# Sparse attention of the two later mixers: groups taken one by one, or in pairs around halves of the merge gates

## The reference, cut to what matters

```python
def nsa_mixer(q, kv, gate_logits, cmp_pos, cmp_w1, cmp_w2):   # 8 heads = 2 kv x 4, d = 64, S = 256
    ...                                   # kc, vc: 15 compressed keys and values
    def block_fn(qb):                     # 128 queries
        p_c = masked_softmax(q . kc - slope * dist)           # compressed branch
        o_c = p_c . vc
        ...                               # 16 blocks selected of 4: all of them
        p_s = masked_softmax(q . ks - slope * dist);  o_s = p_s . vs   # selected branch
        p_w = masked_softmax(q . kw - slope * dist);  o_w = p_w . vw   # window branch
        return g[..., 0:1] * o_c + g[..., 1:2] * o_s + g[..., 2:3] * o_w
...
g_a, g_b, g_c = split(sigmoid(h @ w_merge_gate[l] + b_merge_gate[l]), 3)   # 1024 x 3072
mix = g_a * (y_a @ w0) + g_b * (y_b @ w1) + g_c * (y_c @ w2)
```

## Time and profile before

| | |
|---|---|
| median of 3 runs | 1881.63 us (1881.41 to 1882.01) |
| the profiled execution | 1882.02 us; span 1880.2 us |
| PE busy | 1863.6 us (99%) |
| PEld busy | 1601.1 us (85%) |
| DVE busy | 1340.4 us (71%) |
| ACT busy | 861.0 us (46%) |
| POOL busy | 124.3 us (7%) |
| DMA | 343.46 MB, mean 183 GB/s |
| TensorE clock granted, mean | 0.999 of full |

### The profile page before, as it was taken

How to read it: one execution, slowest core, us unless ns; L and a number is a source line. 1 busy time by engine, 2 the same in 40 slices (tenths; PEclk the granted TensorE clock), 3 DMA queues, 4 the chain that set the end, 5 groups by cost and what they waited for, 6 DMA issues and landing times.

```text
span 1880.2 us, 28201 instructions
## 1 busy us (share of the span) xinstructions
PE 1863.6 (99%) x10664; PEld 1601.1 (85%) x10664; DVE 1340.4 (71%) x1697; ACT 861.0 (46%) x1107; POOL 124.3 (7%) x155
## 2 busy tenths in 40 slices
PE   9999999999999999999999999999999999999998
PEld 8998888888888888888977888888888897788887
DVE  5676767776767776776876677677777767677777
ACT  5554434474334444344375433443335337644333
POOL 1001200230000100000300100010000020000000
PEclk9999999999999999999999999999999999999999
DMA  7423555425555565544434465556554444455453
GB/s 307 180 90 148 199 181 187 171 82 203 212 191 188 224 223 200 181 167 169 178 137 162 175 227 184 201 218 229 197 182 175 164 166 168 147 189 213 180 199 113
DMA packets 48548, 343.46 MB, mean 183 GB/s; under 512 B 5472, under 2 KB 5504, under 8 KB 8784
## 3 DMA queue, kind: packets, MB, share of 16 engines
q1 hardware_dynamic: 43200, 310.92, 45.5%
q0 software_dynamic: 5264, 31.35, 4.4%
HBM read 341.20 MB, written 1.05 MB: 182 GB/s over the span
## 4 chain that ended last, share of the span: by engine, by line
PE 66%; issue 0%; DVE 0%; POOL 0%; ACT 0%; DVEq 0%; POOLq 0%
PE bank L1068 16%; PE bank L856 12%; PE bank L858 12%; PE bank L857 12%; PE bank L1067 7%; PE bank L919 2%; PE bank L1070 1%; PE bank L1147 1%; PE bank L1519 1%; PE bank L964 1%; PE bank L959 1%; PE bank L960 1%; PE bank L1443 0%; PE bank L1381 0%; PE bank L1508 0%
## 5 line engine op out<-in xcount | busy, mean ns | idle before, releaser
L2065 DVE TENSOR_TENSOR wlo<-raw,whi 128x2048 fp32r<-128x2048 f32 x292 | 672.1, 2304 | 223.2 <-ACT whi L1586 222.7
L1586 ACT ACTIVATE whi<-raw 128x2048 fp32r<-128x2048 f32 x293 | 559.3, 1910 | 256.4 <-PE bank L858 252.3
L1068 PE MATMUL bank<-ysp,whi 128*128 128x512 f32 x1920 | 666.1, 396 | 0.0
L1067 PE MATMUL bank<-ysp,wlo 128*128 128x256 f32 x1680 | 468.6, 279 | 0.0
L1068 PEld LDWEIGHTS bank<-ysp,whi 128*128 128x128 f32 x1920 | 347.7, 188 | 67.0
L1067 PEld LDWEIGHTS bank<-ysp,wlo 128*128 128x128 f32 x1680 | 316.8, 189 | 10.7
L1669 ACT ACTIVATE sg<-sg 128x256 f32<-128x256 f32 x120 | 50.2, 418 | 468.2 <-DVE sg L2262 468.2
L856 PE MATMUL bank<-whi,ysp 128*128 128x512 f32 (+3 forms) x592 | 217.3, 367 | 0.3 <-DVE wlo L2065 0.3
L858 PE MATMUL bank<-whi,ysp 128*128 128x512 f32 (+3 forms) x592 | 212.8, 359 | 0.0
L857 PE MATMUL bank<-wlo,ysp 128*128 128x512 f32 (+3 forms) x592 | 212.4, 359 | 0.0
L856 PE MATMUL bank<-whi,hl 128*128 128x512 f32 x528 | 206.0, 390 | 0.0
(11 more groups left out here) (359 smaller groups left out, 2356.7 us busy)
## 6 DMA issues: line engine op xcount, KB each, us to landing
raw<-stream SPq DMA_DIRECT2D x294, 1024.0 KB, 4.8
sr<-side POOLq DMA_DIRECT2D x10, 1024.0 KB, 5.2
gbc<-gains POOLq DMA_DIRECT2D x11, 512.0 KB, 3.9
cw<-small POOLq DMA_DIRECT2D x2, 2048.0 KB, 10.7
gbias<-gate_rows POOLq DMA_DIRECT2D x6, 512.0 KB, 4.3
dbias<-dilb POOLq DMA_DIRECT2D x1, 2304.0 KB, 12.8
lng<-rows POOLq DMA_DIRECT2D x2, 1024.0 KB, 5.2
tab<-second POOLq DMA_DIRECT2D x1, 1724.0 KB, 15.0
```

Source lines behind the costliest of these rows:

```text
L1067: pe.matmul(o[:, 0, :], lo[:, k, cols], yh[:, k, :], start=False, stop=False, skip_group_check=True)
L1068: last = pe.matmul(o, hi[:, k, cols], ysp[:, :, k, :], start=k == 0, stop=k == 7)
L1586: act.activation(whi[s], raw[s], ACT.Copy).then_inc(hi_made, 1)
L2065: dve.tensor_tensor(wlo[s], raw[s], whi[s].bitcast(F32), ALU.subtract).then_inc(lo_made, 1)
```

## The change

The stage's own order replaces `attention` on all three engines. TensorE, for k from 0 to 4: scores of the two groups of pair k (with one wait, for the maxima of all groups of the pair before), gate half 2+2k, turning of both groups of pair k-1, gate half 3+2k, value sums of both groups of pair k-1. ACT: split of tile 4+2k, copies of pair k-1, tanh of half 2+2k, exponentials of group 2k, split of tile 5+2k, exponentials of group 2k+1, scaling of both, tanh of half 3+2k; for k = 3 the high part of the first output (`out_high(0)`) comes first. DVE: split of tile 4+2k, (k = 0: maxima of groups 0 and 1), sum of gate half 2+2k, copies of pair k-1, (k = 1 to 3: maxima of pair k), shares of group 2k, sum of gate half 3+2k, split of tile 5+2k, shares of group 2k+1. Buffers, banks, amounts of work and the code of each step stay as they were.

```diff
--- before.py
+++ after.py
@@ -1492,9 +1492,6 @@
                 square(B, plan.tb["ya"], lambda m, k: uA[:, m, k * P:k * P + P], 4, 8)
                 pe.wait_ge(ro_used, l + 1)
 
-                def gate_step(i):
-                    gate_half(2 + i, i < 2)
-
                 def compressed_out(m):
 
                     if m == 0:
@@ -1520,7 +1517,39 @@
                                              start=False, stop=i % 4 == 3 and kt == m, tile_position=(0, r), skip_group_check=True)
                     return last
 
-                attention(B, "nsa", nsa_groups(), AG_NSA + 8 * l, gate_step, summed=values_summed)
+                groups, ag = nsa_groups(), AG_NSA + 8 * l
+                tb_nsa = [plan.tb["nsa"] + (i if i < 4 else 2 * i - 4) for i in range(9)]
+
+                def pair_scores(k):
+
+                    pe.wait_ge(mx_ready, ag + 2 * k)
+                    for i in (2 * k, 2 * k + 1):
+                        g = groups[i]
+                        for h in range(4):
+                            o = pb[2 + 2 * (i % 2) + h // 2][:, (h % 2) * S:(h % 2) * S + g["nk"]]
+                            last = pe.matmul(o, g["q"][h], g["k"][h], start=True, stop=True)
+                        last.then_inc(sc_done, 1)
+
+                def pair_T(k):
+
+                    for i in (2 * k, 2 * k + 1):
+                        g, nt = groups[i], groups[i]["nk"] // P
+                        for b in range(nt):
+                            hs = range(4) if nt == 1 else (2 * b, 2 * b + 1)
+                            pe.wait_ge(p_ready, 2 * (ag + i) + (2 if nt == 1 else b + 1))
+                            batch(B, tb_nsa[i] + b, [g["p"][:, h, kt * P:kt * P + P] for h in hs for kt in range(nt)])
+
+                for k in range(5):
+                    if k < 4:
+                        pair_scores(k)
+                    gate_half(2 + 2 * k, k == 0)
+                    if k:
+                        pair_T(k - 1)
+                    gate_half(3 + 2 * k, k == 0)
+                    if k:
+                        for i in (2 * k - 2, 2 * k - 1):
+                            copied(B, tb_nsa[i + 1])
+                            values_summed(i).then_inc(o_done, 1)
 
                 tb = plan.tb["y"]
                 pe.wait_ge(yb_ready, l + 1)
@@ -1998,13 +2027,46 @@
                     act.wait_ge(o_done, AG_NSA + 8 * l + 4 * m + 4)
                     act.activation(cTh[m], pb[1].rearrange("p (h q) -> p h q", h=4), ACT.Copy).then_inc(oT_hi, 1)
 
-                def beside(i):
-
-                    if i == 6:
+                groups, ag = nsa_groups(), AG_NSA + 8 * l
+                tb_nsa = [plan.tb["nsa"] + (i if i < 4 else 2 * i - 4) for i in range(8)]
+
+                def exps(i):
+
+                    g = groups[i]
+                    act.wait_ge(mx_ready, ag + i + 1)
+                    for h in range(4):
+                        p = g["p"][:, h, 0:g["nk"]]
+                        ins = act.activation(p, p, ACT.Exp, bias=nmx[:, i % 2, h:h + 1], accum_out=den[:, i % 4, h:h + 1])
+                    ins.then_inc(p_made, 1)
+
+                def scaled(i):
+
+                    g = groups[i]
+                    act.wait_ge(share_ready, 8 * l + i + 1)
+                    for h in range(4):
+                        p = g["p"][:, h, 0:g["nk"]]
+                        ins = act.activation(p, p, ACT.Copy, scale=share[:, i % 2, h:h + 1])
+                        if h % 2:
+                            ins.then_inc(p_ready, 1)
+
+                for k in range(5):
+                    if k == 3:
                         out_high(0)
-                    ahead(B, "gates", 2 + i)
-
-                attention(B, "nsa", nsa_groups(), AG_NSA + 8 * l, beside, lambda i: gate_tanh(2 + i), shared=8 * l)
+                    ahead(B, "gates", 2 + 2 * k)
+                    if k:
+                        for i in (2 * k - 2, 2 * k - 1):
+                            if i >= 2:
+                                act.wait_ge(o_done, ag + i - 1)
+                            for b in range(groups[i]["nk"] // P):
+                                plain_T(B, tb_nsa[i] + b, pt_part(groups[i], b))
+                    gate_tanh(2 + 2 * k)
+                    if k < 4:
+                        exps(2 * k)
+                        ahead(B, "gates", 3 + 2 * k)
+                        exps(2 * k + 1)
+                        scaled(2 * k)
+                        scaled(2 * k + 1)
+                        gate_tanh(3 + 2 * k)
                 ahead(B, "gates", 11)
                 gate_tanh(11)
 
@@ -2774,21 +2836,47 @@
                     dve.wait_ge(oT_hi, M * l + m + 1)
                     dve.tensor_tensor(cTl[m], pb[1].rearrange("p (h q) -> p h q", h=4), cTh[m].bitcast(F32), ALU.subtract).then_inc(oT_lo, 1)
 
-                def beside(i):
-
-                    if i == 6:
+                ag = AG_NSA + 8 * l
+                tb_nsa = [plan.tb["nsa"] + (i if i < 4 else 2 * i - 4) for i in range(8)]
+
+                def maxima(i):
+
+                    g, nk_ = groups[i], groups[i]["nk"]
+                    dve.wait_ge(sc_done, ag + i + 1)
+                    dve.wait_ge(p_ready, 2 * (ag + i) - 2)
+                    if i >= 2:
+                        dve.wait_ge(tb_done, B.tb0 + tb_nsa[i - 2] + groups[i - 2]["nk"] // P)
+                    for h2 in range(2):
+                        src = bank2(2 + 2 * (i % 2) + h2)[:, :, 0:nk_]
+                        ins = dve.tensor_tensor(g["p"][:, 2 * h2:2 * h2 + 2, 0:nk_], src, g["bias"][h2], ALU.add)
+                    link(ins)
+                    link(dve.tensor_reduce(mx[:, i % 2, :], g["p"][:, :, 0:nk_], AX_X, ALU.max))
+                    dve.tensor_scalar(nmx[:, i % 2, :], mx[:, i % 2, :], -1.0, None, ALU.mult).then_inc(mx_ready, 1)
+
+                for k in range(5):
+                    if k == 3:
                         out_low(0)
-                    if i % 2 or i >= 8:
-                        gate_sum(2 + i)
-                        if i < 8:
-                            shares(groups[i], i)
-                        ahead(B, "gates", 2 + i)
-                    else:
-                        ahead(B, "gates", 2 + i)
-                        gate_sum(2 + i)
-                        shares(groups[i], i)
-
-                attention(B, "nsa", groups, AG_NSA + 8 * l, None, beside)
+                    ahead(B, "gates", 2 + 2 * k)
+                    if k == 0:
+                        maxima(0)
+                        maxima(1)
+                    gate_sum(2 + 2 * k)
+                    if k:
+                        for i in (2 * k - 2, 2 * k - 1):
+                            if i >= 2:
+                                dve.wait_ge(o_done, ag + i - 1)
+                            for b in range(groups[i]["nk"] // P):
+                                plain_T(B, tb_nsa[i] + b, pt_part(groups[i], b))
+                    if 0 < k < 4:
+                        maxima(2 * k)
+                        maxima(2 * k + 1)
+                    if k < 4:
+                        shares(groups[2 * k], 2 * k)
+                    gate_sum(3 + 2 * k)
+                    if k < 4:
+                        ahead(B, "gates", 3 + 2 * k)
+                        shares(groups[2 * k + 1], 2 * k + 1)
+                ahead(B, "gates", 11)
                 tb = plan.tb["y"]
                 square_T(B, tb, 2, bTl, bTh)
                 b0 = plan.step["branch"]
```

## The result

The changed kernel takes 1903.08 us (median of 4 runs, 1900.77 to 1903.87) against 1881.74 us of before; the ratio is 1.0112, 95% interval 1.0099 to 1.0124. It is slower by 21 us. The profiled execution took 1900.77 us, span 1899.0.

A forecast was written before the change was run, and what follows sets the result against it. TensorE, busy 99% of the span, was taken as the bound. Stages 9.15 us longer per layer (18.3) on 1882.02 gave 1900.3, median 0.4 lower; clock falls of 3.4 us made 1903, range 1894 to 1911.

The forecast's parts named there:

- both stages without the clock: Stage in both layers, clock kept up: each 9.15 us longer, 18.3 us for two.
- the clock: TensorE's clock drops to half pace in stalls of 3 us: 1.7 us a fall, one counted per layer, 3.4 us.
- The order on ACT and DVE: Splits stand ahead of work TensorE needs; it waits about 3, 3.4 and 3.3 us at three places a layer.
- (a): Gate half 3+2k shares bank 0, waits for DVE's sum of half 2+2k; about 3 us at gate half 5.
- (b): From pair 2, turning's third and fourth batches wait for ACT's and DVE's copies; stalls 3.4 us (pair 2), 3.3 (pair 3).
- Pair 3's stall: TensorE's wait in the turning of pair 3: 3.3 us, able to swallow a clock fall in pair 2's stall.
- Wait (c): Scores of a pair wait for maxima of the pair before; not late, maxima done at 6.2 us, scores after 6.8.
- The switches: Fewer switches on TensorE save 0.3 us per each of four pairs plus 0.3, about 1.5 us a layer (0 to 4.5).
- Not slower: Rival, 5%: the order fits, turning waits shrink to the bank's turn-round, 2.4 us in all, switches pay 3.0: 1881 us.
- The clock falls in every stall: Rival, 15%: the clock drops in all three stalls a layer, loss behind pair 3 adding 3.4 us: 1907 us.

The follow-up runs named there:

- the first run: Changed kernel with DVE's split of tile 4+2k moved behind the gate sum and copies in loops 1, 3 and 4: 1888.78 us, ratio 1.0038.
- the third: Changed kernel with ACT's split of tile 4+2k moved ahead of the scaling, for k from 1: 1893.27 us, ratio 1.0063.
- the fourth: The order in step: changed kernel with ACT and DVE reordered, TensorE's pairs kept: 1880.72 us, ratio 0.9996 to the kernel before.

## Why the prediction was right

It said 1903 us, slower; 1903.08 was measured. The path it walked is right piece by piece; that the total agrees to a tenth is in part luck, since its last two terms were off in opposite directions. Step by step, with the measured moments moved by the 0.22 us by which this stage began sooner:

| step | forecast | measured |
|---|---|---|
| gate half 5 starts | 956.2 | 956.13 |
| turning of pair 1 done | 972.4 | 972.33 |
| turning of pair 2 done | 992.1 | 991.75 |
| turning of pair 3 done | 1011.3 | 1010.91 |
| stage ends | 1018.9 | 1018.43 |
| both stages without the clock | +18.3 | +17.4 (86.06 + 86.05 kept busy in all waits, less 154.68) |
| the clock | +3.4 | +3.9 (the rest of 1903.08 - 1881.74) |

*The order on ACT and DVE.* Waits (a) and (b) came where they were forecast and for the reason given: the first run shows it by taking DVE's split out of the way, the third by making ACT's sooner, the fourth by both. Pair 3's stall was 1.8 us, not 3.3, because the late end of gate half 9 used up the rest, as forecast for a fall there; with the clock kept up it was 3.4 (fourth batch 3.10 us behind the third). Wait (c), the scores, was not late. ACT's idle time ahead of the first tanh was to be some 6 us:

```profile
942.61 0.64 ACT L2010 ACTIVATE gates<-gates 128x512 f32<-128x512 f32 x1 [6.24 <-DVE gates L2805]
```

*The switches* were put too low. By an estimate from the order in step (76.87 us, less two turn-rounds of 0.6 and two waits of 0.15 at the gate halves) a layer with TensorE unhindered would take 75.4, so the pairs save 2.0 us, not 1.5. The chains hide that in the changed kernel: the piece that TensorE paces, from gate half 5 to the end of pair 1's turning, took 16.20 us against the 16.2 of the forecast.

*The clock* was the weakest step. The prediction took the price of a fall from TensorE's pace at the beginning of the span, where the earlier trace rows itself gives a granted clock of 1.00; the changed kernel's trace shows the lower clock directly. Windows over the beginning of gate half 9 in the first layer and of gate half 5 in the second:

```profile
991.60:995.00 3.40, 3.40 (x11) 2.67 (x10) 3.09 (x4) 0.00 (x0) 0.00 (x0) 0.53 0.72 292
1585.80:1589.20 3.40, 3.01 (x7) 2.46 (x8) 3.30 (x9) 1.56 (x6) 0.00 (x0) 0.51 0.58 222
```

Half speed, the 1.2 GHz level, in both. In this execution it fell at gate half 9 in both layers (swallowed) and at gate half 5 in the second layer alone: 6.92 us against 5.53, so 1.4 us a fall, where I took 1.7. That is why the two stages differ by 1.43, and it is one fall that counts where the forecast had two. The kernel's other runs are 1.9 to 3.1 us longer, at a mean granted clock of 0.994 to 0.995 and not 0.997, and with TensorE kept busy in all waits that spread is gone: so the clock fell oftener in them. At 1.4 us a fall the 3.9 us of the median are nearly three falls (an estimate; which ones, no trace shows). The forecast's 3.4 came of too high a price and too low a count, and stages put 0.9 us too long made up for what was missing.

*The rivals.* "Not slower" failed for the reason given against it, though its sums held: the order in step proves that the work fits (1880.72 measured, 1881 in the rival). "The clock falls in every stall" did not hold in the profiled execution. Of its four stalls of some 3 us (gate half 5 and pair 2, in each layer) three brought the clock down; the two of pair 3 were shorter, 1.8 us, and brought none. In the longer runs it may have come nearer to holding. The Trainium skill ("TensorE: Matmul & The Clock Gate", section "Why this matters for your kernels") asks for no idle gaps between bursts of matmuls, so that the throughput does not drop. The trace agrees in three of the four stalls; in the fourth, gate half 5 of the first layer, it does not: 2.98 us of waiting there left the clock up, 2.97 us at the same place of the second layer brought it down.

## What to carry to other kernels

On engines that run in strict order, the place of an instruction that may wait counts for more than its length: look at what stands behind it and who needs that. A split for a tile that is needed 10 us later must not stand ahead of the sum that another engine waits for. When the strings of several engines are made longer by pairing work, walk one round of them on the clock of the old trace, start to start; that gave the end of every piece here within 0.5 us. And a delay that a later wait takes up costs nothing by itself, like the slow gate half 9 ahead of pair 3's stall, while a repair in one place can uncover the next wait, as at gate half 7.

## What had not been expected

The clock is what makes this kernel's time vary: 1900.77 to 1903.87 us with idle waits, 1899.02 to 1900.05 with TensorE busy in them, though 27 matmuls a layer were added. Filling the waits with work that nobody reads was worth 3.3 us here (4.0 by the spans). And falls differ in size: with ACT's split ahead of the scaling, the fall behind pair 2 made gate half 9 longer by 1.6 us in one layer and by 2.4 us in the other. Nor did it take a stall of 3 us: with the turnings one by one, the clock fell behind a wait of 1.9 us in the first layer, and did not behind the same wait in the second.
